# A two-block transformer in fp32 on one core: the relative bias written once and turned over on TensorE, the first norms' sums moved to VectorE inside the modulation loop, and GpSimd's low parts made in quarters

## The reference

```python
for l in range(2):                      # first block
    sh1, sc1, gt1, sh2, sc2, gt2 = split(silu(c) @ w_ada[l] + b_ada[l], 6)    # also for c_ctx
    h  = rms_norm(x, g_norm1[l]) * (1 + sc1) + sh1       # the same for ctx -> hc
    ...                                  # h @ w_in[l]: three kinds of attention over x and ctx
    x  = x + gt1 * (concat([oa, ob, oc]) @ w_out[l])
    x  = x + gt2 * conv_ffn(rms_norm(x, g_norm2[l]) * (1 + sc2) + sh2)
for l in range(2):                      # second block
    mix = hybrid_mixer(x)               # x @ w_in_2: conv, top-k attention, banded attention with
    ...                                 #   bias = rel_bias[:, clip(i - j + pad, -63, 128) + 63]
    x = layer_norm(ALPHA * x + mix); x = layer_norm(ALPHA * x + cross(x, mem)); x = layer_norm(ALPHA * x + mlp(x))
```

## Time and profile before

| | |
|---|---|
| median of 3 runs | 3930.71 us (3928.43 to 3932.87) |
| profiled execution, its own time | 3927.56 us |
| span in that profile | 3925.8 us |
| PE busy | 3604.0 us, 92% |
| DVE, ACT, POOL busy | 47%, 41%, 39% |
| granted PE clock, mean | 0.947 of full |

### The profile page before, as it was taken

How to read it: one execution, slowest core, us unless ns; L and a number is a source line. 1 busy time by engine, 2 the same in 40 slices (tenths; PEclk the granted TensorE clock), 3 DMA queues, 4 the chain that set the end, 5 groups by cost and what they waited for, 6 DMA issues and landing times.

```text
span 3925.8 us, 49519 instructions
## 1 busy us (share of the span) xinstructions
PE 3604.0 (92%) x19550; PEld 2852.4 (73%) x19550; DVE 1853.6 (47%) x2957; ACT 1624.5 (41%) x2662; POOL 1545.0 (39%) x648
## 2 busy tenths in 40 slices
PE   6998878969999999979999897999999989999998
PEld 5865555758888876647888675987887666977886
DVE  4863654422346575663322486534113586353114
ACT  4436644423345545753433235433222335434222
POOL 0534331424457733313444330524444321614442
PEclk7999987989999999979999998999999999999998
DMA  7623221323335642212333330422333221413331
GB/s 211 138 86 103 88 72 29 102 78 97 93 117 165 171 97 83 86 37 86 97 97 90 87 86 8 130 58 76 96 97 95 70 65 38 129 49 86 97 96 60
DMA packets 643986, 357.88 MB, mean 91 GB/s; under 512 B 70469, under 2 KB 616365, under 8 KB 643757
## 3 DMA queue, kind: packets, MB, share of 16 engines
q1 hardware_dynamic: 639598, 345.94, 31.7%
q10 hardware_dynamic: 4159, 8.78, 0.6%
HBM read 346.28 MB, written 8.39 MB: 90 GB/s over the span
## 4 chain that ended last, share of the span: by engine, by line
PE 80%; DVE 8%; ACT 4%; issue 3%; DMA 2%; POOL 2%; SPq 1%; ACTq 0%; DVEq 0%
PE psum L790 62%; PE psum L942 5%; PE psum L966 3%; PE psum L984 2%; PE psum L862 2%; POOL w_lo L770 1%; ACT work L1331 1%; DVE neg_max L1745 1%; PE psum L1013 1%; PE psum L893 1%; ACT w_hi L1195 1%; PE psum L829 1%; DMA w_raw<-in_w_up_dram 1%; PE psum L912 1%; PE psum L991 1%
## 5 line engine op out<-in xcount | busy, mean ns | idle before, releaser
L770 POOL TENSOR_TENSOR w_lo<-w_raw,w_hi 128x1024 fp32r<-128x1024 f32 (+1 forms) x626 | 1521.7, 2434 | 2286.6 <-ACT w_hi L1195 2286.4
L790 PE MATMUL psum<-h_hi,w_hi 128*128 128x512 f32 (+1 forms) x3024 | 1163.9, 385 | 115.4 <-POOL w_lo L770 49.3
L790 PE MATMUL psum<-h_lo,w_hi 128*128 128x512 f32 (+1 forms) x3024 | 1128.2, 373 | 0.0
L790 PE MATMUL psum<-h_hi,w_lo 128*128 128x512 f32 (+1 forms) x3024 | 1126.7, 373 | 0.0
L1195 ACT ACTIVATE w_hi<-w_raw 128x1024 fp32r<-128x1024 f32 (+1 forms) x626 | 654.9, 1047 | 767.6 <-PE psum L790 630.3
L790 PEld LDWEIGHTS psum<-h_hi,w_hi 128*128 128x128 f32 x3024 | 582.5, 193 | 264.8 <-issue 57.2
L790 PEld LDWEIGHTS psum<-h_lo,w_hi 128*128 128x128 f32 x3024 | 584.9, 193 | 99.9 <-issue 8.9
L790 PEld LDWEIGHTS psum<-h_hi,w_lo 128*128 128x128 f32 x3024 | 583.7, 193 | 98.0
L790 PE MATMUL psum<-hid_hi,w_hi 128*128 128x512 f32 (+1 forms) x1040 | 390.7, 376 | 2.7 <-POOL w_lo L770 2.7
L790 PE MATMUL psum<-hid_lo,w_hi 128*128 128x512 f32 (+1 forms) x1040 | 389.4, 374 | 0.0
L790 PE MATMUL psum<-hid_hi,w_lo 128*128 128x512 f32 (+1 forms) x1040 | 389.4, 374 | 0.0
(11 more groups left out here) (213 smaller groups left out, 3953.4 us busy)
## 6 DMA issues: line engine op xcount, KB each, us to landing
w_raw<-in_w_up_dram SPq DMA_DIRECT2D x132, 512.0 KB, 3.8
w_raw<-in_w_ff_dram SPq DMA_DIRECT2D x128, 512.0 KB, 4.0
w_raw<-in_w_in_dram SPq DMA_DIRECT2D x92, 512.0 KB, 3.9
w_raw<-in_w_ada_dram SPq DMA_DIRECT2D x80, 512.0 KB, 3.9
w_raw<-in_w_down_dram SPq DMA_DIRECT2D x48, 512.0 KB, 4.1
w_raw<-in_w_mkv_dram SPq DMA_DIRECT2D x32, 512.0 KB, 4.0
w_raw<-in_w_down_dram SPq DMA_DIRECT2D x24, 384.0 KB, 3.4
w_ada_first<-in_w_ada_dram SPq DMA_DIRECT2D x4, 2048.0 KB, 23.5
```

What stands on the lines that cost most here:

```text
L770: nc.gpsimd.tensor_tensor(WL[:, c % NSPLIT, 0:nk, :], RAW[:, c % NRAW, 0:nk, :], WH[:, c % NSPLIT, 0:nk, :].bitcast(F32), ALU.subtract).th ...
L790: m = pe.matmul(out_ap, lhs(a, k), rhs(b, k), start=(k == 0 and n == 0), stop=(k == nk - 1 and n == 2))
```

## The change

1. *Relative bias.* `REL_PAD` becomes 12 rows of 384 (18 KB), written by one DMA. ACT's queue reads it with a step of +1, so that the rows come out in reverse order; PE multiplies by a reversed identity `FLIP` (three fp32 matmuls of 512 columns per layer, at steps 13 to 15 of `mix_in`), and DVE copies the low half and adds the mask to the high half out of PSUM (three pairs, steps 14 to 16) in place of six adds at step 19.
2. *Start.* `x` and `ctx` are turned inside the modulation loop, after steps 3, 3, 3, 3, 4 and 5. Squares are made on ACT at steps 6 to 13, two per step; DVE adds them up (`add_square`), and PE makes only one set of one-column matmuls per stream (`rms_stat`). Rows of the modulation are copied and turned block by block in the loop. The late parameters, the head gains (now one instruction) and the lambda sums come after the first norm; the exponential of lambda comes after the projection of `x`. `gain_rows` moves to SP ahead of the fourth `w_ada` block, `rest_of_rows` to SP behind it and ahead of the first `w_in` chunks, and the write of `RPB_PAD` to ACT's queue at step 4 of the loop.
3. *Quarters.* For `w_in` and `w_in_2` POOL makes each low part in four instructions of 128x256.

```diff
@@ sync @@
             for i in range(4):
+                if i == 3:
+                    sp.wait_ge(*at("turned", "first_rows"))
+                    gain_rows()
                 w = A["w_ada"][0, :, i * 4 * P:(i + 1) * 4 * P].rearrange("(k p) n -> p k n", p=P)
                 sp.dma_start(WA[:, i, :, :], w).then_inc(*mark(f"ada_in{i}", "first", 16))
...
+            rest_of_rows()
...
-                if c in rel[20:24]:
-                    n = 3 * (c - rel[20])
+                if c == rel[20]:
                     sp.wait_ge(*at("zeroed", "rel"))
-                    sp.dma_start(REL_PAD[n:n + 3], RELR[n:n + 3, :].unsqueeze(1).broadcast_to([3, P, 384])).then_inc(
-                        *mark("rel_written", "last" if n == 9 else n, 16))
+                    sp.dma_start(REL_PAD[:, :], RELR[:, :]).then_inc(*mark("rel_written", "last", 16))
+        FIRST_TURNS = (3, 3, 3, 3, 4, 5)
+        def first_squares(n):
+            return [(("n1", "xc"[m // KT], 0), m % KT) for m in (2 * n - 12, 2 * n - 11) if 0 <= m < 2 * KT]
@@ gpsimd @@
-                nc.gpsimd.tensor_tensor(WL[:, c % NSPLIT, 0:nk, :], RAW[:, c % NRAW, 0:nk, :],
-                                        WH[:, c % NSPLIT, 0:nk, :].bitcast(F32), ALU.subtract).then_inc(
-                                            *mark("w_lo", c))
+                step = 2 if name in ("w_in", "w_in_2") else nk
+                for k in range(0, nk, step):
+                    m = nc.gpsimd.tensor_tensor(WL[:, c % NSPLIT, k:k + step, :], RAW[:, c % NRAW, k:k + step, :],
+                                                WH[:, c % NSPLIT, k:k + step, :].bitcast(F32), ALU.subtract)
+                m.then_inc(*mark("w_lo", c))
@@ tensor @@
             for n in range(4 * ADA_FIRST):
                 pe.wait_ge(*at("first_lo", n))
-                ada_product(PS[0:4, 4 + n // 4, :], wide(WH[:, n % NSPLIT]), wide(WL[:, n % NSPLIT]), n % 4)...
-                S, k = ("n1", "xc"[n // KT], 0), n % KT
-                pe.wait_ge(*at("sq_ready", (S, k)))
-                for t in range(TOKENS[S[1]] // P):
-                    m = pe.matmul(PS[:, t, 8 * (n // KT):8 * (n // KT) + 1], SQ4[k % 4][:, t * P:(t + 1) * P], MEAN[:, 0:1], ...
+                r = (n + 2) % NSPLIT
+                ada_product(PS[0:4, 4 + n // 4, :], wide(WH[:, r]), wide(WL[:, r]), n % 4).then_inc(*mark("first_used", n))
+                for i, after in enumerate(FIRST_TURNS):
+                    if after == n:
+                        pe.wait_ge(*(at("x_in", 3) if i < 4 else at("ctx_in", 5)))
+                        turn_in("in", [i])
+                for S, k in first_squares(n - 1):
+                    if k == KT - 1:
+                        rms_stat(S)
+                if n % 4 == 1 and n > 4:
+                    first_turn(n // 4 - 1)
+            first_turn(ADA_FIRST - 1)
...
                     spread(("n1", s, l))
+                    if (s, l) == ("c", 0):
+                        late_params()
...
+                    if CONV_STEP - 4 <= step < CONV_STEP - 1:
+                        pair = step - CONV_STEP + 4
+                        if pair == 2:
+                            pe.wait_ge(*at("bias_step", ("rel", l, 0)))
+                        pe.matmul(PS[:, 6 + pair % 2, :], FLIP, TBK[:, 2 * pair:2 * pair + 2, :], start=True, stop=True)...
@@ scalar @@
+                if n == 4:
+                    act.wait_ge(*at("bias_in", "rpb"))
+                    act.dma_start(RPB_PAD, RPBR[:, :].unsqueeze(1).broadcast_to([120, 64, P])).then_inc(...)
+                for S, k in first_squares(n):
+                    ...
+                    square(S, (XT if S[1] == "x" else CT)[:, k, 0:T], k, at("turned_taken", ("in", 7 if S[1] == "x" else 11)))
+                if n % 4 == 1 and n > 4:
+                    first_row(n // 4 - 1)
+                if n == 4 * ADA_FIRST - 1:
+                    rms_std(("n1", "x", 0))
+                    rms_std(("n1", "c", 0))
             for c in range(AHEAD):
+                act.wait_ge(*at("first_used", 4 * ADA_FIRST - NSPLIT + c))
                 split(c)
+            first_row(ADA_FIRST - 1)
...
-                    act.dma_start(TBK[:, h, :], bass.AP(REL_PAD.tensor, (l * 6 + h) * P * 384 + 127, [[383, P], [1, 256]])
+                    act.dma_start(TBK[:, h, :], bass.AP(REL_PAD.tensor, (l * 6 + h) * 384, [[1, P], [1, 256]]))...
@@ vector @@
             for n in range(4 * ADA_FIRST):
                 dve.wait_ge(*at("first_hi", n))
+                lo("first_lo", n, wide(WL[:, r]), WA[:, n // 4, n % 4 * 2:n % 4 * 2 + 2, :], wide(WH[:, r]))
+                for i, after in enumerate(FIRST_TURNS):
+                    if after == n:
+                        turn_in("in", [i], lambda i: (XT, i) if i < 4 else (CT, i - 4))
+                for S, k in first_squares(n):
+                    if S[1] == "c" and k == 1:
+                        dve.wait_ge(*at("stat_done", ("n1", "x", 0)))
+                    add_square(S, k, TOKENS[S[1]], ACC)
...
+                    if CONV_STEP - 3 <= step < CONV_STEP:
+                        pair = step - CONV_STEP + 3
+                        ps = PS[:, 6 + pair % 2, :].rearrange("p (h c) -> p h c", h=2)
+                        dve.wait_ge(*at("rel_flipped", (l, pair)))
+                        nc.vector.tensor_copy(TBK[:, 2 * pair:2 * pair + 2, 0:P], ps[:, :, 0:P])...
+                        nc.vector.tensor_tensor(TBK[:, 2 * pair:2 * pair + 2, P:2 * P], ps[:, :, P:2 * P],
+                                                CAUSAL.unsqueeze(1).broadcast_to([P, 2, P]), ALU.add)...
```

More of the change, by code:

```diff
@@ L89, in constant_arrays @@
     causal = np.where(i[None, :] // CHUNK <= i[:, None] // CHUNK, 0.0, NEG).astype(np.float32)
-    pack = np.concatenate([eye, mean, blk64, blk32, pair, half_d, half_i, causal, window, freq], axis=1)
+    head = np.tile(np.array([0.125, 1.0, 0.125, 1.0, 32.0 ** -0.5, 1.0], np.float32), (P, 1))
+    pack = np.concatenate([eye, eye[::-1], blk64, blk32, pair, half_d, half_i, causal, window, freq, head, mean[:, :1]], axis=1)
     ca, sa = axial_tables(64)
@@ L344, in build @@
         PS = ctx.enter_context(nc.psum_tensor("psum", [P, 8, 512], F32))
-        IDENT, MEAN, BLK64, BLK32, PAIR, HALF_D, HALF_I, CAUSAL = (PACK[:, i * P:(i + 1) * P] for i in range(8))
+        IDENT, FLIP, BLK64, BLK32, PAIR, HALF_D, HALF_I, CAUSAL = (PACK[:, i * P:(i + 1) * P] for i in range(8))
         WINDOW = PACK[:, 8 * P:8 * P + 64]
         FREQ = PACK[:, 8 * P + 64:8 * P + 66]
+        HEAD_SCALE = PACK[:, 8 * P + 66:8 * P + 72]
+        MEAN = PACK[:, 8 * P + 72:8 * P + 73]
         BLK = (BLK64, BLK32)
@@ L354, in build @@
         PROBS = {width: [WORK[:, width * i:width * (i + 1)] for i in range(4 * 768 // width)] for width in (512, 768)}
[L356 removed]
+        FIRST_ROW = WORK[0:4, 2048 + 3 * P:2048 + 7 * P]
         def prm(name, i):
@@ L461, in _, with gain_rows @@
         def _(sp):
+            def gain_rows():
+                for l in range(DEPTH):
+                    for i, name in enumerate(GAINS):
+                        c = PCOL["gains"][0] + l * len(GAINS) + i
+                        w = A[name].shape[1]
+                        to = PROWS[c % P:c % P + 1, c // P, :].rearrange("p (r w) -> p r w", w=w)
+                        sp.dma_start(to, A[name][l:l + 1, :].unsqueeze(1).broadcast_to([1, P // w, w])).then_inc(
+                            *mark("rows_in", (name, l), 16))
             for i in range(4):
+                if i == 3:
+                    sp.wait_ge(*at("turned", "first_rows"))
+                    gain_rows()
                 w = A["w_ada"][0, :, i * 4 * P:(i + 1) * 4 * P].rearrange("(k p) n -> p k n", p=P)
@@ L821, in tok_sum @@
                 for t in range(n):
-                    m = pe.matmul(PS[:, bank, col + t:col + t + 1], sums[:, t * P:(t + 1) * P], MEAN[:, 0:1], start=True,
+                    m = pe.matmul(PS[:, bank, col + t:col + t + 1], sums[:, t * P:(t + 1) * P], MEAN, start=True,
                                   stop=True)
@@ L1123, in logits @@
                 def logits(step):
+                    if CONV_STEP - 4 <= step < CONV_STEP - 1:
+                        pair = step - CONV_STEP + 4
+                        if pair == 0:
+                            pe.wait_ge(*at("bias2_in", (l, 5)))
+                            pe.wait_ge(*at("rope_step", (("mix_in", l), 7, "sin")))
+                        if pair == 2:
+                            pe.wait_ge(*at("bias_step", ("rel", l, 0)))
+                        pe.matmul(PS[:, 6 + pair % 2, :], FLIP, TBK[:, 2 * pair:2 * pair + 2, :], start=True, stop=True).then_inc(
+                            *mark("rel_flipped", (l, pair)))
                     for n in index_logits(step):
@@ L1200, in split_ahead @@
                     split(c + AHEAD)
-            def gain_rows():
-                for l in range(DEPTH):
-                    for i, name in enumerate(GAINS):
-                        c = PCOL["gains"][0] + l * len(GAINS) + i
```

(8 more changed lines are left out.)

139 lines of the change are left out of this document (61 added, 78 removed).

## The result

| | before | after |
|---|---|---|
| median, four runs each | 3930.4 us (3928.4 to 3932.9) | 3878.6 us (3877.1 to 3882.4) |
| span of the profiled execution | 3925.8 us | 3877.1 us |
| PE busy | 3604.0 us | 3590.7 us |
| granted PE clock, mean | 0.947 | 0.954 |

The ratio is 0.9875, 95% interval 0.9862 to 0.9887: 1.25% faster. I forecast 3867.5. The whole range (3855 to 3883) holds the time, the forecast's own range (3857 to 3875) doesn't, and the time is rival B's, 3879. The two traces differ by 48.7 us, the medians by 51.8, for a sum of 63. (The median before is of four runs here; ahead of the prediction it was of three, 3930.7.)

The account below looks back on a forecast made before the run. PE was taken as the bound (80% of the chain), with gains only where it stands or works needlessly. Terms -41 - 17 - 6 + 1 = -63 from the median 3930.7 gave 3867.5 us; own range 3857 to 3875, whole range 3855 to 3883.

Parts of the forecast that it names:

- rival B: `mix_in`: turning over costs PE a longer wait at step 15 and more, shorter waits; +5.6 for -6, 3879 us; chance 0.11.
- 1, bias in the feed-forward stage: Feed-forward stage: one 18 KB write replaces four of 590 KB that hold up `w_up` loads; -41, between -30 and -43.
- 2, start: Modulation loop to first `w_in` product: that product starts near 67.0, not 84.60; -17 taken, -13 to -21.
- Rival A: Start bound by DMA: the `RPB_PAD` write delays block 3; gain of 8 for 17, 3876 us; chance 0.15.
- 3, `mix_in`: `mix_in`, both layers: less DVE waiting for POOL against new copies, additions and turnings over; -6, between -14 and +8.
- PE stands there some 5 us: `mix_in` step 15: PE waits for DVE's first pair, covered by 9.9 idle; DVE then waits about 1.4.
- the -2 that I had summed: `mix_in`, per layer: DVE's sum -5 + 1.4 + 1.4, and PE's also -2; between +4 and -5.
- once, early: Early in layer 0's `mix_in`: blocked DVE operations leave the chain, -3, less 0.65 for a longer low part.
- 9.3 us lost: `mix_in`, DVE's busy run: `L2070` loses 2.0, `L2074` 4.2, `L2045` 3.1 to POOL; 5 taken as gained by quarters.
- 4, quarters in the projections: Projections' context tiles: quarters of 0.75 us make a chunk 3.0, perhaps 3.4, against tiles of 3.30; +1.
- rival D: 28 context tiles: POOL becomes the bound at 5.6 us a chunk; 65 us added, 3938 us; chance 0.02.
- C: Feed-forward stage: the single bias write also lands late and holds `w_up` back by 11 us; 3878 us; chance 0.06.

Follow-up runs that it names:

- b_late: The changed kernel with the third turning over moved from step 15 to step 17 on PE, its DVE pair to step 18: 3867.9 us, ratio 0.9847.
- a_again: The changed kernel run again without any edit, as the measure for three experiments beside it: 3877.2 us, ratio 0.987.
- j_after: The changed kernel run once more without any edit, in a later set of runs: 3881.2 us, ratio 0.9881.

## Why the prediction was right in its sign and 11 us off

**1, bias in the feed-forward stage (-41): right.** 40.8 by the stage's own times. What I called the cause, the engines "held up", was right too, but I laid it to the write's bytes among the loads; the one DMA of twelve rows says that its cutting was the larger part.

**2, start (-17): right in its sum, in part by luck.** First product at 67.86 for 67.0, 16.7 earlier. The steps one by one: first block in at 14.2 (13.8), copies done at 28.0 (29.4), steps 4 and 5 in 8.1 (9.2), additions 0.70 (0.69) and 0.43 (0.48), end of the loop at 61.3 (61.4). Two misses cancel in this last one: step 9 ended near 45.5 and not at 48.3, and step 10 then took some 6 us and not 4.1, since DVE had to wait for two products of 1.8, a turning of 1.79 that the sum did not hold there, and the sums of 1.51. The queues were misjudged too: block 3 was taken as landed by 37.6 and landed at 46.8, because `gain_rows` held SP for 19 us. It was needed just then, so the error cost 0.82 us off the chain and nothing in time. Rival A is out: no block after the first stands in the chain. The medians of the later runs show 8 to 12 of it, the traces 17.

**3, `mix_in` (-6): wrong, +7.8.** This is the step that failed, at two places. First, "PE stands there some 5 us, which its 9.9 of idle time covers, and DVE then waits about 1.4": the 5.53 us are right, but the wait has a price of its own that no row of mine held. Behind it the clock fell to 0.68, which made the third turning over, the scores and the next tile 3.4 us longer. And DVE's next scores are late too: DVE stood 3.73 us at the next step, not 1.4, and DVE's list bounds the end of the stage, so the idle time there could not cover all of PE's wait. On PE the sum is 3.8 of turning over + 5.5 + 2.2 of slower work = 11.5 added, 9.90 - 2.53 = 7.4 given by the end, +4.1 for a measured +4.4. With the wait gone (`b_late`) the layers come to -1.7 and -2.3, the -2 that I had summed: so the sum without the wait's price fits. Second, the "once, early" -2.4: the blocked 2.80 us operation is gone and nothing came of it, since the chain there now goes over the sines to the first low part, in four quarters:

```profile
2174.32 1.05 ACT w_hi L1231
2175.44 3.02 POOL w_lo L788 x4
```

12 and 2.4 are the 14 that the term was off; the sum with them is 49, and the traces say 48.7 (the medians 51.8). That it closes so well is in part luck, since single stages move by 4 us between traces and the term is 10.2 and 8.1 in the other two traces of the changed kernel.

*POOL and DVE in this term.* Of the 9.3 us lost I took 5 as regained. Gained in layer 0 were about 7.7 (`L2111` 0.8, `L2115` 4.2, `L2086` 2.7) and given back 4.1 (`L2090` 1.6, `L2093` 0.8, the copy 1.65), 3.6 in all. "An operation waits for one quarter at most" was false for the copy. POOL's timeline of that moment:

```profile
2273.36 2.83 POOL L788 TENSOR_TENSOR w_lo<-w_raw,w_hi 128x256 fp32r<-128x256 f32 x4 [5.14 <-ACT w_hi L1231]
...
2284.41 4.31 POOL L788 TENSOR_TENSOR w_lo<-w_raw,w_hi 128x256 fp32r<-128x256 f32 x4 [2.60 <-ACT w_hi L1231]
...
2300.74 2.40 POOL L788 TENSOR_TENSOR w_lo<-w_raw,w_hi 128x1024 fp32r<-128x1024 f32 x1 [3.04 <-ACT w_hi L1231]
```
```profile
2301.35 1.87 DVE L2137 COPY sel_mask<-const_sb 128x128 f32<-128x128 f32 x1
```

At the end of the stage POOL already works on `mix_out`'s weights, whose chunks stay whole: the copy starts 0.6 into one and ends 0.08 after it. The rows above it show the other side: beside the convolution four quarters took 4.31, where they took 2.83 while DVE was picking the largest scores. The Trainium skill (SBUF — State Buffer, "SBUF: two separate sides") says that the port pair which GpSimd shares with a DVE operation of two SBUF inputs, or in a 2-port mode, is an exclusive lock for a whole instruction of whoever comes first. The 1.87 for a copy that ends with POOL's 2.40 us instruction, and the 4.31 for 2.83, agree with it.

**4, quarters in the projections (+1): right, and nothing was to be measured.** Context tiles still stand 3.30 apart, and rival D needed a chunk of 5.4, where four quarters took 2.83 when nothing held them up (2.40 whole; I had taken 3.0):

```profile
95.17 2.87 PE psum L808 x24
98.04 0.43 PE psum L915 x2
```

**Rivals.** B was nearest, in time (3879, with +5.6 for this term where +7.8 was measured) and in half of its mechanism: what the turning over added on PE, 11.5, was more than the end gave, 7.4. But the wait itself was of the length forecast, and the clock stands in the place of "more, shorter waits". I gave it 0.11; that an added wait of over 5 us stood in the sum as free was reason for more. C is out: behind the small write SP issues the loads of `w_up` without a stop.

## What to carry to other kernels

An idle time at the end of a stage doesn't pay for a wait in its middle: ask what the waiting engine feeds. Here a 5.5 us wait on PE cost 6 us per layer although 9.9 stood idle 45 us later, because it also made the bounding engine late and lowered the clock; moving one turning over by two steps gave it back. When small copies of a row are written many times over, look at the number of rows in one DMA before its bytes. And for a few us, compare the stages of several traces and repeat the medians: one set of runs said 14 for an edit for which a second set said 2.

## What the runs showed of the hardware that was not expected

- After a wait of 5.5 us on PE the granted clock had a mean of 0.68 over the next 10.6 us (0.71 in `a_again`); six filling matmuls in the same wait kept it at 1.00.
- Four 590 KB writes of three rows each cost 40.8 us of a stage, one 2.36 MB write of twelve rows 13.5.
- One issue of a small load on SP took 9.03 us behind three 2 MB loads (9.69 in `a_again`), the same kind of issue 0.56 later.
- A 128x128 copy on DVE with both sides in SBUF took 1.87 us beside a 2.40 us instruction of POOL, and 0.23 without (2.47 beside it in `j_after`); four quarters of POOL took 4.31 us beside DVE's convolution, and 2.83 beside its picking of the largest.
- Executions of one kernel moved by up to 4.3 us in single stages, at a few places each time. What sets these moves stays open.
